# Decoding several heads' picks at once in 16-bit integers, six row buffers, stores from ScalarE's queue, three row steps per head

## The reference

```python
q = (hf @ w_query).reshape(T, 8, 2, 128)
scores = jnp.einsum('thcd,hcnd->thcn', q, sub_keys)       # 8 heads x 2 x 128 keys
s1, i1 = lax.top_k(scores[:, :, 0], 16); s2, i2 = lax.top_k(scores[:, :, 1], 16)
cand_s = s1[..., :, None] + s2[..., None, :]              # 16 x 16 pairs
cand_i = i1[..., :, None] * 128 + i2[..., None, :]
top_s, pos = lax.top_k(cand_s, 16)                        # the 16 best pairs
idx = take_along_axis(cand_i, pos); gates = softmax(top_s)
act = gelu(einsum('thkd,td->thk', expert_u[idx], x))      # 128 picks per token
out = einsum('thk,thkd->td', gates * act, expert_v[idx])  # of 16384 experts
```

## Time and profile before

| what | us |
|---|---|
| median of 3 runs | 3160.67 (3160.18 to 3161.33) |
| profiled execution, its own time | 3167.87 |
| its span, first to last instruction | 3166.1 |
| VectorE busy | 2447.6 (77%) |
| TensorE matmuls busy | 2802.2 (89%) |
| ScalarE busy | 1264.7 (40%) |
| GpSimd busy | 1097.2 (35%) |

### The profile page before, as it was taken

The page is one execution under the profiler, slowest core; times in us unless marked ns, Lnnn a source line. Parts: engine busy times, 40 slices in busy tenths (PEclk is TensorE's granted clock), DMA queues, the critical chain, the costliest instruction groups (busy, mean ns, idle before and its releaser), DMA issues. The chain is left out here.

```text
span 3166.1 us, 43207 instructions
## 1 busy us (share of the span) xinstructions
PE 2802.2 (89%) x15167; PEld 2445.5 (77%) x15167; DVE 2447.6 (77%) x4426; ACT 1264.7 (40%) x2390; POOL 1097.2 (35%) x778
## 2 busy tenths in 40 slices
PE   7999788989988998989988888886899999999998
PEld 4779455767778888889988888886777777877776
DVE  4512567459999998888888665665999999999998
ACT  4111456221221478877777783112222222222222
POOL 0000000001113343433334554553556555555552
PEclk9999678989998999999999999998999999999999
DMA  6710000323327777777777888998999999999997
GB/s 260 265 40 2 28 0 27 106 82 103 105 94 242 236 277 245 266 266 261 275 260 270 313 315 327 331 321 290 371 378 386 366 385 374 375 376 377 384 384 274
DMA packets 309138, 794.29 MB, mean 251 GB/s; under 512 B 26592, under 2 KB 125568, under 8 KB 304896
## 3 DMA queue, kind: packets, MB, share of 16 engines
q0 software_dynamic: 110592, 402.70, 35.9%
q1 hardware_dynamic: 197248, 385.62, 33.9%
q10 hardware_dynamic: 1152, 4.19, 0.3%
HBM read 694.11 MB, written 98.30 MB: 250 GB/s over the span
## 5 line engine op out<-in xcount | busy, mean ns | idle before, releaser
L92 POOL DMA_INDIRECT fetched<-u_rows,row_index x384 | 560.5, 1460 | 928.2 <-DVE row_act L110 842.8
L378 PE MATMUL ps_up<-h_hi,col_hi 128*128 128x320 f32 (+1 forms) x2288 | 571.2, 331 | 157.9 <-DVE col_lo L469 74.5
L92 POOL DMA_INDIRECT fetched<-v_cols,row_index x384 | 532.8, 1387 | 412.6 <-DVE row_sum L115 370.0
L110 DVE CUSTOM_DVE_ANT_0 fetched<-fetched,h_rows_then_gates 128x1024 f32<-128x1024 f32 x384 | 470.4, 1225 | 188.7 <-DMA fetched<-u_rows,row_index 149.9
L378 PE MATMUL ps_up<-h_hi,col_lo 128*128 128x320 f32 (+1 forms) x2288 | 557.6, 325 | 4.9 <-issue 4.9
L378 PE MATMUL ps_up<-h_lo,col_hi 128*128 128x320 f32 (+1 forms) x2288 | 558.3, 325 | 0.0
L378 PEld LDWEIGHTS ps_up<-h_hi,col_hi 128*128 128x128 f32 x2288 | 397.9, 195 | 182.7 <-issue 159.9
L115 DVE SCALAR_TENSOR_TENSOR row_sum<-fetched,row_act,row_sum 128x1024 f32<-128x1024 f32 x381 | 487.7, 1280 | 41.9 <-DMA fetched<-v_cols,row_index 39.7
L761 PE MATMUL ps_y<-v_hi,coef_hi 128*128 128x512 f32 x1280 | 406.9, 400 | 77.7 <-DVE coef_lo L836 75.0
L378 PEld LDWEIGHTS ps_up<-h_hi,col_lo 128*128 128x128 f32 x2288 | 400.5, 194 | 16.3 <-issue 5.2
L378 PEld LDWEIGHTS ps_up<-h_lo,col_hi 128*128 128x128 f32 x2288 | 401.8, 195 | 11.4
(11 more groups left out here) (236 smaller groups left out, 3699.0 us busy)
## 6 DMA issues: line engine op xcount, KB each, us to landing
stage<-cols SPq DMA_DIRECT2D x144, 512.0 KB, 6.2
stage<-v_cols SPq DMA_DIRECT2D x128, 512.0 KB, 7.8
expert_act<-stage SPq DMA_DIRECT2D x128, 320.0 KB, 6.1
expert_gate<-g_buf SPq DMA_DIRECT2D x20, 2048.0 KB, 12.0
stage<-expert_act SPq DMA_DIRECT2D x128, 320.0 KB, 6.3
g_raw<-expert_gate SPq DMA_DIRECT2D x64, 320.0 KB, 10.0
h_rows_then_gates<-expert_gate SPq DMA_DIRECT2D x64, 320.0 KB, 9.5
z_n<-w_ada SPq DMA_DIRECT2D x32, 512.0 KB, 6.6
```

The lines of the kernel that those rows point to most:

```text
L92: nc.gpsimd.indirect_dma_start(self.buf[:, n % NBUF], None, rows, bass.IndirectOffsetOnAxis(ap=self.at[:, tile, k:k + 1], axis=0)).then_in ...
L110: nc.vector.tensor_tensor_reduce(out=row, in0=row, in1=self.h[:, tile], scale=1.0, scalar=0.0, op0=ALU.mult, op1=ALU.add, accum_out=pick). ...
L378: mm = pe.matmul(ps_up[:, b, half, 0:width], w[:, b, k], h[:, k, a:a + width], start=(k == 0 and i == 0), stop=(k == DC - 1 and i == 2))
```

## The change

The two halves of `route` become two functions: `best_keys(sc, i)` puts its result in slot `i` of a set, and `best_pairs(n, ...)` forms, searches and decodes the pairs of `n` sets together: the three row tiles of a head, or two heads of a dense tile (every fourth slot). Key numbers and positions are unsigned 16-bit; comparison and product write 16-bit values into the space of `cand`, and one reduce sums them. The row index of all three tiles is written by one operation with one semaphore. Row buffers go from 4 to 6. Each routing head does three row steps, and the last 32 slots 3, 3, 4, 3 instead of 4, 3, 4, 3. ScalarE's queue issues the stores of `act_d` (in the next slot, after `hi`) and of `gate_d`. The copy that reuses `g_buf` stands behind the second gates of its slot. In the diff the removed lines of `route`'s second half and of `row_head` are left out; they are L490 to L531 above.

```diff
-NBUF = 4
+NBUF = 6
 PICKS = HEADS * TOPK
-HEAD_STEPS = 2
+HEAD_STEPS = 3
 GROUPS = ND * P // GT
 LAG = 19
+SETS = max(2, NG)
 HELD = min(ND, 4) - (ND > 4)
 
...
@@ -85,7 +87,7 @@
     def fetch(self, pool, nc, n):
         table, tile, k = self.step(n)
         if table == 0 and k % TOPK == 0:
-            pool.wait_ge(self.index_ready[tile], k // TOPK + 1)
+            pool.wait_ge(self.index_ready, k // TOPK + 1)
...
@@ -119,7 +121,7 @@
 def row_schedule():
 
 
-    per_slot = [2] * 16 + [2, 3] * 32 + [4] * 16 + [4, 3] * 16
+    per_slot = [2] * 16 + [2, 3] * 32 + [4] * 16 + [3, 3, 4, 3] * 8
     done, steps, gelu_at = HEAD_STEPS * HEADS, [], None
     for e, want in enumerate(per_slot):
...
@@ -178,16 +180,17 @@
+        iota_k = sb("iota_k", [P, TOPK], U16)
         work = sb("work", [P, 2, NKEY])
-        top = sb("top", [P, 2, TOPK])
-        topi = sb("topi", [P, 2, TOPK], U32)
-        topf = sb("topf", [P, 2, TOPK])
-        cand = sb("cand", [P, TOPK, TOPK])
+        top = sb("top", [P, 2, SETS, TOPK])
+        topi = sb("topi", [P, 2, SETS, TOPK], U16)
+        cand = sb("cand", [P, SETS, TOPK, TOPK])
         cand2 = sb("cand2", [P, TOPK, TOPK])
-        best = sb("best", [P, TOPK])
-        pos = sb("pos", [P, TOPK], U32)
-        pos2 = sb("pos2", [P, 2, TOPK], U32)
-        pick = sb("pick", [P, 2, TOPK, TOPK])
+        best = sb("best", [P, SETS, TOPK])
+        pos = sb("pos", [P, SETS, TOPK], U16)
+        pos2 = sb("pos2", [P, 2, SETS, TOPK], U16)
+        pick = cand[:].rearrange("p i a b -> p (i a b)").bitcast(U16).rearrange("p (k a) -> p k a", a=TOPK)
+        row_idx = sb("row_idx", [P, 2, SETS, TOPK])
         idx = sb("idx", [P, 2, PICKS])
         shifted = sb("shifted", [P, PICKS])
...
@@ -253,11 +256,6 @@
...
-            def gates_out(blk):
-
-                sp.wait_ge(g_copied, 4 * blk + 4)
-                sp.dma_start(gate_d[blk], g_buf[:]).then_inc(g_stored, 16)
-
             next_scores(0)
             next_scores(1)
             for e in range(ETILES):
@@ -266,14 +264,10 @@
                 if e % 2 and e // 2 + 2 < ND * HEADS:
                     next_scores(e // 2 + 2)
                 g = e - LAG - 1
-                if 0 <= g < GROUPS and g % 4 == 3:
-                    gates_out(g // 4)
                 if g == GROUPS + 4:
                     sp.wait_ge(g_stored, 16 * (GROUPS // 4))
                     for part in gate_parts(gate_d, 0):
                         sp.dma_start(g_raw[0][:, part[0]].rearrange("p b j t -> p b (j t)"), part[1]).then_inc(g_in[0], 16)
-                sp.wait_ge(res_done, e + NQ + 1)
-                sp.dma_start(act_d[e], res[:, e % 2, 0:TD]).then_inc(res_out[e % 2], 16)
 
             sp.wait_ge(lo_done, NQ + ETILES)
...
@@ -339,11 +333,22 @@
 ...
-            act.wait_ge(consts, 2)
+            def gates_out(blk):
+
+                act.wait_ge(g_copied, 4 * blk + 4)
+                act.dma_start(gate_d[blk], g_buf[:]).then_inc(g_stored, 16)
+
+            def act_out(e):
+                act.wait_ge(res_done, e + NQ + 1)
+                act.dma_start(act_d[e], res[:, e % 2, 0:TD]).then_inc(res_out[e % 2], 16)
+
+            act.wait_ge(consts, 3)
             for e in range(ETILES):
                 n, b = e + NQ, e % 2
                 if n + 1 <= last_n:
                     next_hi(n, b, n // 2)
+                if e:
+                    act_out(e - 1)
                 if e == 2:
                     act.wait_ge(tile_routed, 1)
                     nc.scalar.activation(rows.gate[:], rows.gate[:], ACT.Exp).then_inc(exp_done, 1)
@@ -353,15 +358,21 @@
                     nc.scalar.activation(expd[:].rearrange("p h k -> p (h k)"), shifted[:], ACT.Exp).then_inc(exp_done, 1)
                 if e == gelu_at:
                     rows.gelu(act, nc)
-                if 0 <= e - LAG - 1 < GROUPS:
-                    gates_copy(e - LAG - 1)
-                if 0 <= e - LAG + 1 < GROUPS:
-                    second_gates(e - LAG + 1)
+                copied, made = e - LAG - 1, e - LAG + 1
+                if 0 <= copied < GROUPS and copied % 4:
+                    gates_copy(copied)
+                if 0 <= made < GROUPS:
+                    second_gates(made)
+                if 0 <= copied < GROUPS and copied % 4 == 0:
+                    gates_copy(copied)
+                if 0 <= e - LAG - 1 < GROUPS and (e - LAG - 1) % 4 == 3:
+                    gates_out((e - LAG - 1) // 4)
                 act.wait_ge(up_done, n + 1)
                 if e >= 2:
                     act.wait_ge(res_out[b], 16 * (e // 2))
                 nc.scalar.activation(res[:, b, 0:TD].rearrange("p (a t) -> p a t", a=2), ps_up[:, b, :, 0:HD],
                                      ACT.Gelu_apprx_tanh).then_inc(res_done, 1)
+            act_out(ETILES - 1)
 
         @block.tensor
...
@@ -468,7 +480,8 @@
...
-            def route(sc, idx_out, shifted_out):
+            def best_keys(sc, i):
+
 
                 ch.sync()
                 for r in range(2):
@@ -477,68 +490,67 @@
                     for c in range(2):
                         if r == 1:
                             ch.sync(1)
-                        ch.done(nc.vector.max(top[:, c, lo8], src[c]))
+                        ch.done(nc.vector.max(top[:, c, i, lo8], src[c]))
                     for c in range(2):
                         ch.sync(1)
-                        ch.done(nc.vector.max_index(topi[:, c, lo8], top[:, c, lo8], src[c]))
+                        ch.done(nc.vector.max_index(topi[:, c, i, lo8], top[:, c, i, lo8], src[c]))
                     if r == 0:
                         for c in range(2):
-                            ch.done(nc.vector.match_replace(work[:, c], top[:, c, lo8], src[c], LOWEST))
+                            ch.done(nc.vector.match_replace(work[:, c], top[:, c, i, lo8], src[c], LOWEST))
                 ch.sync()
                 dve.sem_inc(head_read, 1)
+
+            def best_pairs(n, idx_out, shifted_out):
+
+
+                ch.done(nc.vector.tensor_tensor(cand[:, 0:n], top[:, 0, 0:n].unsqueeze(3).to_broadcast([P, n, TOPK, TOPK]),
+                                                top[:, 1, 0:n].unsqueeze(2).to_broadcast([P, n, TOPK, TOPK]), ALU.add))
+                ch.sync()
                 flat2 = cand2[:].rearrange("p a b -> p (a b)")
+                for i in range(n):
+                    flat = cand[:, i].rearrange("p a b -> p (a b)")
+                    ch.done(nc.vector.max(best[:, i, 0:8], flat))
+                    ch.sync()
+                    ch.done(nc.vector.max_index(pos[:, i, 0:8], best[:, i, 0:8], flat))
+                    ch.done(nc.vector.match_replace(flat2, best[:, i, 0:8], flat, LOWEST))
+                    ch.sync()
+                    ch.done(nc.vector.max(best[:, i, 8:16], flat2))
+                    ch.sync()
+                    ch.done(nc.vector.max_index(pos[:, i, 8:16], best[:, i, 8:16], flat2))
+                    ch.sync()
+                ch.done(nc.vector.tensor_tensor(shifted_out, best[:, 0:n], best[:, 0:n, 0:1].to_broadcast([P, n, TOPK]), ALU.subtract))
+                ch.done(nc.vector.tensor_scalar(pos2[:, 0, 0:n], pos[:, 0:n], 4, None, ALU.logical_shift_right))
+                ch.done(nc.vector.tensor_scalar(pos2[:, 1, 0:n], pos[:, 0:n], 15, None, ALU.bitwise_and))
                 ch.sync()
+                m = n * TOPK
+                for c in range(2):
+                    at = pick[:, c * m:c * m + m]
+                    ch.done(nc.vector.tensor_tensor(at, pos2[:, c, 0:n].rearrange("p i k -> p (i k)").unsqueeze(2).to_broadcast([P, m, TOPK]),
+                                                    iota_k[:].unsqueeze(1).to_broadcast([P, m, TOPK]), ALU.is_equal))
                 ch.sync()
+                for c in range(2):
+                    at = pick[:, c * m:c * m + m].rearrange("p (i k) a -> p i k a", k=TOPK)
+                    ch.done(nc.vector.tensor_tensor(at, at, topi[:, c, 0:n].unsqueeze(2).to_broadcast([P, n, TOPK, TOPK]), ALU.mult))
                 ch.sync()
+                ch.done(nc.vector.tensor_reduce(idx_out, pick[:, 0:2 * m].rearrange("p (c i k) a -> p c i k a", c=2, k=TOPK), AX.X, ALU.add))
                 ch.sync()
+
+            dve.wait_ge(consts, 3)
 
             for u in range(HEADS):
                 lo(2 * u + 2)
                 dve.wait_ge(sc_copied, 2 * u + 2)
-                row_head(0, u)
-                lo(2 * u + 3)
-                for tile in range(1, NG):
-                    if u == HEADS - 1 and tile == NG - 1:
-                        lo(2 * u + 4)
-                    row_head(tile, u)
+                for tile in range(NG):
+                    best_keys([sc_out[:, c, tile] for c in range(2)], tile)
+                    if tile == 0:
+                        lo(2 * u + 3)
+                if u == HEADS - 1:
+                    lo(2 * u + 4)
+                at = slice(u * TOPK, u * TOPK + TOPK)
```

(56 more changed lines are left out.)

1 line of the change is left out of this document (removed).

## The result

The changed kernel takes 3005.62 us (median of four runs, 3001.64 to 3008.63) where the kernel before takes 3161.0 beside it: ratio 0.9507 [0.949, 0.9523], 155 us less. The forecast was 3039 us, 122 less. The profiled execution of after has a span of 3004.1 us against 3166.1.

A forecast was written before the change was run, and what follows sets the result against it. Five stretches with different limits: VectorE and TensorE in routing, VectorE and the gate store's loop in slots 24 to 83, row buffers after, VectorE nearly full in down. 0 - 6 - 44 - 18 - 34 - 20 = -122, 3039 us, range 2978 to 3100.

The forecast's parts named there:

- Decoding: VectorE's decode of a pair: 9.91 us instead of 11.00, with 16-bit operations priced like 32-bit ones.
- Routing: Eight heads: VectorE 28.4 us, period 28.7, a wait of 8 us once for first rows; net 0, from -10 to +8.
- Slots 24 to 83: Fifteen gate groups: VectorE's and gate loops both near 38, coupled at 39.0 for 41.9 us a group; -44 us.
- rival D: Gate groups: ScalarE's store issues aren't hidden, gate loop 41 us, only 13 instead of 44 us gained; 3070 us, chance 0.16.
- the 8.4 us between copy and issue are a wait in SP's order: Gate groups: the store stands in SP's queue behind a load that waits for VectorE's `lo`; 8.4 us.
- Slots 0 to 23: VectorE per four slots falls from 31.1 to 30.0 us; six groups, -6 us.
- Slots 84 to 127: Six buffers lift the row cap: slots 84 to 99 at 39.5 us a group, -18; slots 100 to 127 at 7.35 each, -34.
- theory L: Rows, mainly past slot 84: four buffers held fetches back by latency, six end that; back to four gives about 3085 us.
- Down: Down stretch, only buffers change: 7.2 us a slot at 390 GB/s over 118 slots; -20 us, from +15 to -50.
- A: Row fetches: transfers, not latency, pace the rows, so the buffers buy nothing; -60 us, 3100 us, chance 0.14.
- B: More comes free: half-price 16-bit operations, gate groups 37.5, slots 84 to 99 at 36, down at 7.0; 2965 us, chance 0.14.
- C: Down stretch: six outstanding gathers delay SP's loads, a slot takes 8.65 us, +148 us; 3207 us, chance 0.06.

The follow-up runs named there:

- old_decode: The kernel before with everything but the batch decode (one head at a time, 32-bit): 3043.98 us, 0.9621.
- better2: Changed kernel, row steps per head 0, 3, 3, 3, 3, 4, 4, 4, and eight steps moved from four gate-group slots to the last 32: 2992.34 us, 0.9463.
- sp_stores: The changed kernel with both stores back in SP's queue in the old order, new place of the reusing copy kept: 3001.63 us, 0.9495.
- before_gates: The kernel before with the reusing copy moved behind the second gates and both stores on ScalarE's queue: 3115.38 us, 0.9871.
- buf4: The changed kernel with four row buffers instead of six: 3065.7 us, 0.9691.
- half_rows: The changed kernel with the 384 fetches of the second table bringing half a row, 2 KB instead of 4 KB per partition: 2955.3 us, 0.9346.
- better: The changed kernel with row steps per head 0, 3, 3, 3, 3, 4, 4, 4, none in the first head: 2994.01 us, 0.9465.
- before_buf6: The kernel before with six row buffers and nothing else: 3104.36 us, 0.9837.

## Why the prediction was right or wrong

**Decoding: right, a little dear.** The pair came out at 9.23 for 9.91 us and `old_decode` costs 38 us. I priced 16-bit operations like 32-bit ones. The multiply, all operands in unit steps, is cheaper: 0.38 us for 512 elements, the compare 0.65. The 32-bit compare and multiply of before:

```profile
1329.67 0.69 DVE L509 TENSOR_TENSOR pick<-pos,iota 128x512 f32<-128x512 uint32 x1
1330.39 0.69 DVE L513 TENSOR_TENSOR pick<-pick,topf 128x512 f32<-128x512 f32 x1
```

The Trainium skill ("VectorE: DVE Perf Modes", Mode 2x_1P) asks for 16-bit operands with step 1 for the double rate. The trace agrees: 0.38 us for the operation that meets this, 0.65 for the one that doesn't. As an estimate by that rule the pair would have been 9.4 us.

**Routing: the terms right, one left out.** VectorE's head (28.6 for 28.7) and the wait for the first rows (7.6 for 8) came as worked out, the stretch -3.4 for 0. What I didn't price was the choice in it: with two steps per head the stretch would have been 12 us shorter. I credited the eight moved rows to slots 100 to 127, and there they were worth nothing.

**Slots 24 to 83: mechanism right, size too small, one reason wrong.** "Both loops near 38; they couple, so I take 39.0" is the term that was mis-sized: 565.2 / 15 = 37.7 us a group. VectorE's loop was forecast at 37.2 + 0.9 = 38.1 and is 37.4 (149.5 / 4), 0.7 less, as the pair is. The other 0.9, for the coupling with the gate loop, had nothing to stand on once that loop was gone as a bound. It isn't shortened to 37: the store is issued 2.39 us after the copy's end, not behind second gates that run until 1134.5 (I had put 6.5 between), and 15 waits of 115.2 us became 10 of 9.9. The forecast also started from 41.9 where the gelus give 42.2. What is left is VectorE: it waits 3.0 us for `col_hi`, a dearer decode costs its full price (`old_decode`), and fewer row steps give theirs back (`better2`). That ScalarE would pay for its issues (rival D) isn't seen: the 0.34 us stand beside activations.

TensorE is a close second. Its slots can follow each other 8.82 us apart, 4 x 8.82 = 35.28 us, which is under VectorE's 36.55. Measured at the gelus, most groups therefore take 35.0 to 38.4 us and every fourth, in which a tile is turned, 41.3 to 42.1: TensorE catches up in the former and waits in the latter. VectorE's own four groups are 149.5 - 4 x 36.55 = 3.3 us longer for the turn, and not 5 or 6.

The wrong reason is "the 8.4 us between copy and issue are a wait in SP's order". The earlier trace rows showed it for the first store, and I took it for all. In the gate groups of before most are 4.4 us and every fourth is 1.2. And SP in the old order does as well once VectorE isn't late (`sp_stores`: 1.2 to 3.0 us). The Trainium skill's rule ("DMA: Bandwidth & Descriptors", Issuing engines are not separate DMA queues), that more issuing engines only save issue time, would have given 0 for ScalarE's queue; in the changed kernel the runs agree with it, and I set it aside on one row. On the kernel before, the stores alone were worth 31 us. An order without SP's wait for VectorE fits the part in the gate groups (22 us in the profiled execution); the part behind slot 100 stays open.

**Slots 0 to 23: -12.4 for -6.** The wait of 10.07 us for the first store fell in this stretch, and I had counted all of them behind it. `before_gates`, without the new decode, gains 9.2 us here, and `old_decode` gives 5.7 back.

**Slots 84 to 127: right, as theory L.** 34.95 us a group at 388 GB/s for 39.5, and 190.1 / 27 = 7.04 us a slot, TensorE's own, for 7.35. I had put a margin on both, for a gate loop and for queued transfers that didn't come. That slots 84 to 99 came out near all the same (-21.5 for -18) is in part luck: the 43.9 us that I started from are the spacing of the stores, and by the gelus these four groups took 161.3 / 4 = 40.3: three took 41.6 to 45.6 and the last, in which the gates end, 29.7. TensorE is busy 136 of 140 us there and the DMA share is 1.00, so which of the two sets that pace isn't told apart. With four buffers 37 us of both stretches come back (`buf4`, profiled execution).

**Down: a transfer bound as said, the size in part by luck.** -20.8 for -20, at 384 GB/s for the 390 assumed. From one `v_hi` to the next a slot fell from 7.28 to 7.18 us, about 13 us over the stretch, not from 7.4 to 7.2. Another 6 us lie ahead of its first slot, where I had counted nothing. `half_rows` shows transfers as the bound; in `better` and `better2` too the stretch stays at 962 and 965 us.

**The rivals.** A fell with `before_buf6` and `buf4`. B was half right: its gate groups at 37.5 and its slots 84 to 99 at 36 came, its half-price operations for the multiply alone, and its down stretch not at all. C didn't come: the end is shorter. D didn't come.

The parts alone, each on the kernel before or undone in the changed one, are 45 (gates), 56 (buffers) and 38 (decode): 139 of 155. The first two are each uncertain by some 10 us, so that the parts help each other isn't shown in the total. In the gate groups it would be plausible: the store's wait and VectorE's sum stood at nearly one length, and taking either alone stops at the other.

More than six row buffers, and the batch decode with 32-bit indices, weren't tried.

## What to carry to other kernels

Where an issue is late, look first at why its queue's earlier entry waits: a late engine, not the queue, may be the cause, and one instruction's delay doesn't stand for all of its kind. Of each stretch compute the sum of every engine, and add a margin for two coupled loops only if both will still be there. A busy share near 100% doesn't name the engine that sets the pace; see which one waits for no other, and what an added or removed operation on it costs. Work moved into another stretch is a gain only if the stretch that it leaves was bound by it, and costs in full where the engine of the new stretch has no gap.

## What the runs showed of the hardware

Two more outstanding gathers of 512 KB, and nothing else, took a slot behind slot 100 from 8.60 to 7.47 us (`before_buf6`, 3.5 rows a slot); taking them from the changed kernel took it from 7.04 to 7.67 (`buf4`, 3.25 rows). With six buffers one core held 388 GB/s over 140 us and 384 over 840 us. A DMA issue on ScalarE's queue (0.34 us) ran ahead of activations that stand before it in the program and still ran 3 us later, and beyond the noise the kernel took no longer than with the stores in SP's queue. On VectorE a 16-bit multiply in unit steps ran at 0.38 us for 512 elements, a 16-bit compare with one operand broadcast along its innermost axis at 0.65, like 32-bit ones (0.69).
